# Recurrence gates of a two-block model: off-diagonal tiles as 64-row products in pairs

## The reference

```python
u = rmsnorm(x, norm_g) @ w_in                       # 1024 -> 2 x 1536
xb, gate = u[..., :1536], u[..., 1536:]
xb = causal_depthwise_conv(xb, conv_w, conv_b)      # 4 taps
xs = xb.reshape(bsz, seq, 16, 96)                   # 16 blocks of 96 channels
r = sigmoid(einsum('bshi,hij->bshj', xs, wr) + br)  # block-diagonal gates
i = sigmoid(einsum('bshi,hij->bshj', xs, wi) + bi)
log_a = -8 * r * softplus(-lam)
a, b = exp(log_a), sqrt(-expm1(2 * log_a)) * (i * xb)
hs = scan(h = a * h + b)                            # along the sequence
x = x + (hs * silu(gate)) @ w_out                   # 1536 -> 1024
```

## Time and profile before

| | us |
|---|---|
| timed runs, three | 1236.79, 1246.23, 1293.43 |
| median | 1246.23 |
| span of the profiled execution | 1260.7 |
| TensorE busy in it | 1197.7 (95%) |
| VectorE busy | 638.9 (51%) |
| GpSimd busy | 487.3 (39%) |
| ScalarE busy | 423.4 (34%) |

### The profile page before, as it was taken

The page is one execution under the profiler, slowest core; times in us unless marked ns, Lnnn a source line. Parts: engine busy times, 40 slices in busy tenths (PEclk is TensorE's granted clock), DMA queues, the critical chain, the costliest instruction groups (busy, mean ns, idle before and its releaser), DMA issues. The chain is left out here.

```text
span 1260.7 us, 16244 instructions
## 1 busy us (share of the span) xinstructions
PE 1197.7 (95%) x5829; PEld 982.8 (78%) x5829; DVE 638.9 (51%) x1129; ACT 423.4 (34%) x838; POOL 487.3 (39%) x489
## 2 busy tenths in 40 slices
PE   6999999999799999995999999998899999999998
PEld 5888888888698878884777667777688888888887
DVE  6869777595657535157356654443732131231221
ACT  5374495452456412221335633332221020110110
POOL 0000000003423349695060041102967677776772
PEclk9999999999899999997996987858899999999999
DMA  6323232223101013331020020100323223232221
GB/s 245 117 96 98 74 117 84 100 93 125 67 18 35 18 34 117 100 118 67 18 84 17 1 67 1 34 1 11 114 93 100 93 91 100 100 100 96 87 100 50
DMA packets 27278, 97.17 MB, mean 77 GB/s; under 512 B 3024, under 2 KB 3408, under 8 KB 27088
## 3 DMA queue, kind: packets, MB, share of 16 engines
q1 hardware_dynamic: 27216, 96.32, 22.7%
HBM read 94.21 MB, written 2.10 MB: 76 GB/s over the span
## 5 line engine op out<-in xcount | busy, mean ns | idle before, releaser
L443 POOL TENSOR_TENSOR hold<-hold 128x2 f32<-128x2 f32 x117 | 26.1, 223 | 698.5 <-PE bank L916 698.5
L914 PE MATMUL bank<-xh,wh 128*128 128x512 f32 x568 | 230.4, 406 | 18.2 <-DVE xl L1514 14.9
L915 PE MATMUL bank<-xl,wh 128*128 128x512 f32 x568 | 224.3, 395 | 0.0
L916 PE MATMUL bank<-xh,wl 128*128 128x512 f32 x568 | 224.1, 395 | 0.0
L914 PE MATMUL bank<-yh,wh 128*128 128x512 f32 x520 | 205.1, 394 | 7.0 <-POOL wl L447 4.9
L915 PE MATMUL bank<-yl,wh 128*128 128x512 f32 x520 | 204.4, 393 | 0.0
L916 PE MATMUL bank<-yh,wl 128*128 128x512 f32 x520 | 204.2, 393 | 0.0
L447 POOL TENSOR_TENSOR wl<-raw,wh 128x512 fp32r<-128x512 f32 x117 | 176.3, 1507 | 0.0
L446 POOL TENSOR_TENSOR wl<-raw,wh 128x512 fp32r<-128x512 f32 x117 | 156.5, 1338 | 9.8
L914 PEld LDWEIGHTS bank<-xh,wh 128*128 128x128 f32 x568 | 108.6, 191 | 42.7 <-issue 14.2
L916 PEld LDWEIGHTS bank<-xh,wl 128*128 128x128 f32 x568 | 108.5, 191 | 23.3
(11 more groups left out here) (210 smaller groups left out, 1837.4 us busy)
## 6 DMA issues: line engine op xcount, KB each, us to landing
raw<-weight_units SPq DMA_DIRECT2D x173, 512.0 KB, 3.5
x<-x_in SPq DMA_DIRECT2D x4, 512.0 KB, 8.1
out_fm<-x SPq DMA_DIRECT2D x8, 256.0 KB, 2.0
arena<-tables SPq DMA_DIRECT2D x1, 1024.0 KB, 10.7
par<-params SPq DMA_DIRECT2D x1, 166.0 KB, 2.4
arena<-swa_table SPq DMA_DIRECT2D x1, 128.0 KB, 11.6
ident<-identity SPq DMA_DIRECT2D x1, 64.0 KB, 9.3
```

The source lines that it names most:

```text
L443: pool.tensor_tensor(hold[:], hold[:], hold[:], ALU.add).then_inc(held, 1)
L914: pe.matmul(out, lh, rh, start=start, stop=False)
L915: pe.matmul(out, lh, rl, start=False, stop=False)
L916: return pe.matmul(out, ll, rh, start=False, stop=stop)
```

## The change

In `gate_products` the three diagonal tiles of r and then of i are done first, with all 128 rows. The four off-diagonal tiles follow as products of 64 rows: (1,0) on the upper partitions and (0,1) on the lower ones form a pair, (2,1) and (1,2) the other. Within a pair the six products are issued in turn, upper, lower, upper, lower, into two different banks, all added to what the diagonal put there. The order is first pair of r, first pair of i, second pair of r, second pair of i. A new semaphore edge_done makes the second pair wait until the first of the same gate is finished, since both write the middle bank. units_done of r is raised after its second pair, so is that of i. The number of instructions stays: 42 products per group.

```diff
+GATE_EDGES = (((1, 0), (0, 1)), ((2, 1), (1, 2)))
...
+        edge_done = sem("edge_done")
...
             def gate_products(g):
+
+                def operands(r, at, rows):
+                    u, (ki, _) = ri_unit(g, r), at
+                    n, cols = GATE_TILES.index(at), XC[g] + ki
+                    wt = [w[rows, u % RING, n * P:(n + 1) * P] for w in (wh, wl)]
+                    xt = [y[rows, cols, :] for y in (yh, yl)]
+                    return [(wt[0], xt[0]), (wt[0], xt[1]), (wt[1], xt[0])]
+
                 for r in range(2):
-                    u = ri_unit(g, r)
-                    pe.wait_ge(split_done, u + 1)
-                    for n, (ki, o) in enumerate(GATE_TILES):
-                        t = rg_tile(g, "ri"[r], o)
-                        first = n == 0 or GATE_TILES[n - 1][1] != o
-                        if first:
-                            rg_bank(t)
+                    pe.wait_ge(split_done, ri_unit(g, r) + 1)
+                    for i in range(3):
+                        out = rg_bank(rg_tile(g, "ri"[r], i))
                         if r == 0:
-                            pe.wait_ge(xc_ready, 3 * g + ki + 1)
-                        mm = three(B[t % 8][:], tile(wh, u % RING, n), tile(wl, u % RING, n), yh[:, XC[g] + ki, :],
-                                   yl[:, XC[g] + ki, :], first, n == 6 or GATE_TILES[n + 1][1] != o)
-                    mm.then_inc(units_done, 1)
+                            pe.wait_ge(xc_ready, 3 * g + i + 1)
+                        for t, (w, y) in enumerate(operands(r, (i, i), slice(0, P))):
+                            pe.matmul(out, w, y, start=t == 0, stop=False)
+                for e, (upper, lower) in enumerate(GATE_EDGES):
+                    for r in range(2):
+                        if e == 1:
+
+                            pe.wait_ge(edge_done, 2 * g + r + 1)
+                        sides = zip(operands(r, upper, slice(0, HD)), operands(r, lower, slice(HD, P)))
+                        for t, ((wu, yu), (wd, yd)) in enumerate(sides):
+                            pe.matmul(B[rg_tile(g, "ri"[r], upper[1]) % 8][:], wu, yu, start=False, stop=t == 2)
+                            mm = pe.matmul(B[rg_tile(g, "ri"[r], lower[1]) % 8][:], wd, yd, start=False,
+                                           stop=t == 2 and e == 1)
+                        mm.then_inc(units_done if e == 1 else edge_done, 1)
```

## The result

Four runs of the changed kernel took 1258.04, 1265.53, 1265.9 and 1266.0 us, median 1265.72. Four runs of the kernel before took 1236.79, 1245.5, 1246.23 and 1293.43 us. The measured ratio is 1.0165, interval 1.0102 to 1.0228. The forecast was 1246.0, range 1234 to 1265: the result lies 0.7 us above the range, and the whole interval of the ratio lies on the slower side, where I had said "no change" (whether the loss is 2%, it leaves open).

What follows compares the result with a forecast made beforehand. VectorE and ScalarE were taken to bound the recurrence from the third block on; 10.1 us of saved products became 2.8 + 5.5 + 2.3 us of TensorE idle: -0.2 us, median 1246.0, range 1234 to 1265.

Steps and rivals of the forecast that it cites:

- The pace of the recurrence: From the third block on, the VectorE-ScalarE loop sets the recurrence's pace: 45.15 us per group against TensorE's 42.16.
- signs that I had named for being wrong: Line 1615 earlier by over 1 us, a pair over 0.3 us, or the output projection starting after 186 us.
- The pair at one step: In gate blocks, two 64-row products of different halves run at once, costing one full product's step, 0.2267 us.
- Rival B: Pairs in the gate blocks don't overlap: +2.5 us, 1248.7 us; chance 0.08.
- C: Alternating 64-row products drain each other at 0.389 us each, blocks take 13.6 us: +15.6, 1262 us; chance 0.04.
- The change of row mode: Switching TensorE between 128-row and 64-row products and back costs 0.1 to 0.3 us per gate block, taken as 0.2.
- The wait on edge_done: TensorE's wait for its first-edge products before the second pair costs 0; at most 0.25 us for each of two waits.
- What is moved: Later signals in gate blocks cost nothing: r after 6.2 us instead of 4.8, i after 7.0 instead of 9.5.
- the wait for r in group 0: ScalarE gets r at 70.5 instead of 69.0 us, yet sigmoid i can start at 73.97, so the loop keeps its time.
- The clock: Half-clock falls after the first two new TensorE pauses vanish in existing pauses; only one after the third shows, +1.7 us.
- second new pause: TensorE idle after the third gate block, waiting for VectorE's low half of the next gate tile: 5.5 us of new idle.
- Rival D: The clock falls in the output projection after the third pause: +1.5 to +4, about 1248 us; chance 0.18.

Runs made afterwards that it cites:

- the one reordering: Changed kernel with both last-group sigmoids moved ahead of the second projection unit's high half on ScalarE: stretch 197.45 us; six runs, median 1264.32 us.

## Why the prediction was right or wrong

*The pace of the recurrence: right.* The loop of VectorE and ScalarE kept its 45.15 us (85.84 to 176.13). TensorE's waits were 2.25 and 5.18 us, I had said 2.8 and 5.5; it went on at 113.23 and 158.38 us where I had 113.6 and 158.73, and this execution was 0.4 us early. With 10.9 us of TensorE's work taken out the period stayed at 45.15, and it fell only when ScalarE's order was shortened. (The wait that I put at 158.1 began at 158.24.) None of the signs that I had named for being wrong came: line 1615 stayed, a pair took 0.23 us, and the projection started at 184.32. The loss lies behind its start, where I had set no sign.

*The pair at one step: right*, 0.23 us; a block of 7.15 us, forecast 7.0. Rival B (no overlap) and C (each drained) are refuted by the starts 0.01 us apart. The Trainium skill (TensorE: Matmul & The Clock Gate, Part 3, Measured speedup vs the span model) gives 3.07 for four row tiles of 32; the 0.295 us for a pair that the prediction estimated from it isn't what this trace shows for two halves at 512 columns: a pair costs the 0.23 us of one full product. *The change of row mode: too low.* At each side two starts are late, 0.32 and 0.34 us instead of 0.23 (67.99 and 68.33; 70.97 and 71.31 on the way back): 0.4 us for both, where I had given 0.1 to 0.3 and taken 0.2; at this place nothing came of it.

*The wait on edge_done: right.* From the second pair on, the twelve follow one another with 0.22 to 0.24 us through both waits.

*The step that failed is "What is moved".* I wrote that unit r's buffer comes free 1.4 us later and that "the high halves that want them follow these same sigmoids". That is so in the loop, where `high_half(b + 7)` stands behind the sigmoid of r. In the last group it is not: `high_half(U_WOUT + 2)` stands ahead of both sigmoids, and it wants r's buffer. The 1.4 us was wrong there too: it counts from the start of a block, but in block 3 r's last products stand behind the wait for i's low half, which I had priced one paragraph on, for TensorE alone. My own times for block 3 put the release at 183.8 us against 179.9 before, 3.9 later; it came at 183.7 against 180.1. ScalarE was ready for that high half at 181.7, so a release only 1.4 us later would have cost it nothing. It waited 2.08 us, the sigmoids came 1.8 us late, and the projection, from which TensorE is the bound, 2.05 us late; the one reordering gave 1.85 back. I had priced the wait for r in group 0 (where it cost nothing, as forecast: the sigmoid of i started at 73.58 against 73.96, the start being 0.4 early) and not looked up the last group's own lines.

*The clock: right in place.* It fell behind the second new pause or behind both, and the stretch was 199.3 us each time; block 3 began at 176.91, as I had it for a fall. Rival D, at 0.18, didn't come: no fall in the projection in any of five profiles.

*The number.* -0.2 us was forecast for the change, +2.05 is what its stretch lost and +2.9 what the medians show. So the change was forecast 2.2 us too low, and the rest of the miss of 19.7 us isn't the change. The 1265.72 us fell outside of the range because I laid the range around 1246, the median of three runs. I had noted that the profile spans 1260.7 us, and that the runs spread over 57 us; 1260.7 and the 2.1 us around it (a run of 1266.0 us spans 1263.9) is the level where most runs lie, 1260 to 1266 us. The profile was the better witness, and the range should have stood around 1263.

## What to carry to other kernels

Before pricing a saving on the busiest engine, take the period of each loop in that stage from two or three starts of one line: TensorE at 42.16 us and a VectorE-ScalarE loop at 45.15 meant that the next saving on TensorE was worth nothing by itself, and that the loop had to be shortened first (then 7.6 us). When an order is changed, follow the release of each buffer to every place that waits for it, the prologue and epilogue too, since there the order of the other engines differs from the loop's, and ask what the signal itself now stands behind: here unit r's release had come to depend on the split of unit i. And when runs of one program differ by more than the effect sought, measure a stretch in the trace between two fixed instructions, which repeated here to 0.1 us in profiles of one kernel while its total moved by 57.

## What the runs showed that I had not expected

- One program, 78 runs on several chips: 1236.8 to 1293.4 us, in groups with gaps between them (1237 to 1248, 1252 to 1255, 1260 to 1266, 1274 to 1277, 1292 to 1293). It comes from the second attention, whose products took 298 to 336 us in the profiles at a granted clock of 0.93 to 0.80.
- After a change to or from 64 rows not only the first product is late (0.32 instead of 0.23 us) but the one behind it as well (0.33 to 0.34). That second delay isn't peculiar to the change of rows: it stands behind short waits between 128-row products too (186.93 to 187.27 us, 0.34).
- With the change, pauses of TensorE of 3.47 us and more in the recurrence were always followed by a half clock for 3.4 or 6.8 us; of seven pauses of 2.25 to 2.3 us four were, three weren't. In the changed kernel the cost vanished in the next wait for VectorE.
